# Tile-wise norms, keys turned once, a new loading order, and the scan's output normed and turned inside the projections, in a two-block fp32 kernel

## The reference, cut to what matters

```python
u = modulate(rmsnorm(x, norm1_g), sh1, sc1)              # x: 512 tokens; the same for 256 context tokens
p = u @ w_in
q, k, v, a_raw, beta = gdn_inputs(p, conv_w, rows)       # convolution, silu, l2norm of q and k
o = gdn_bidir(...)                                       # gated delta rule, both directions, 8 heads of 128
z = p[..., Z_OFF:F_OFF]
yb = o * rsqrt(mean(o * o, -1) + EPS) * gdn_norm_g * silu(z)      # per head
yb = yb @ w_gdn_out
ya = fourier_mix(p[..., F_OFF:GA_OFF]) @ w_fourier_out
x = x + g1 * ((sigmoid(ga) * ya + sigmoid(gb) * yb) @ w_merge_out)
h2 = modulate(rmsnorm(x, norm2_g), sh2, sc2)
x = rmsnorm(x + g2 * moe_ffn(h2), final_norm_g)
# second block, two layers: norm, projections, three attentions, projection onto x, norm, feed-forward onto x
# and a last rms_norm
```

## Time and profile before

| | us |
|---|---|
| median of three runs (4345.22 to 4346.45) | 4345.42 |
| the profiled execution | 4341.2 |
| its span in the trace | 4339.3 |

### The profile page before, as it was taken

One profiled execution on the slowest core, in us unless ns is written; L12 is line 12 of the kernel. 1 busy time (PEld: TensorE's weight loads), 2 busy tenths in 40 slices (PEclk: granted clock), 3 DMA queues, 4 the chain that ended last, 5 costly groups with the idle time before them and its releaser, 6 DMA issues. The chain is left out here.

```text
span 4339.3 us, 50934 instructions
## 1 busy us (share of the span) xinstructions
PE 3672.8 (85%) x18705; PEld 3094.1 (71%) x18705; DVE 2828.8 (65%) x3496; ACT 1983.2 (46%) x2560; POOL 300.1 (7%) x316
## 2 busy tenths in 40 slices
PE   2988888888966599999999998378789988678998
PEld 1768888875855488888888886356578776566876
DVE  4686666634453599999999997758555333863323
ACT  3432222222221488888888886218422222662221
POOL 0011111100000101101100000120000000200000
PEclk7988999999977799999999999688889999798999
DMA  3333000014522699999999996630156422112322
GB/s 126 116 117 126 0 1 0 0 60 174 184 84 84 249 372 381 382 379 381 380 381 382 379 380 254 219 84 30 39 168 191 125 70 58 22 64 63 97 93 68
DMA packets 264412, 733.57 MB, mean 169 GB/s; under 512 B 38734, under 2 KB 139710, under 8 KB 211782
## 3 DMA queue, kind: packets, MB, share of 16 engines
q1 hardware_dynamic: 250968, 681.54, 43.2%
q0 software_dynamic: 8416, 32.42, 2.2%
q10 hardware_dynamic: 4896, 17.83, 1.0%
HBM read 684.44 MB, written 52.80 MB: 170 GB/s over the span
## 5 line engine op out<-in xcount | busy, mean ns | idle before, releaser
L1844 DVE TENSOR_TENSOR ex_WP_lo<-ex_W,ex_WP_hi 128x2048 fp32r<-128x2048 f32 x408 | 919.1, 2287 | 42.8 <-ACT ex_WP_hi L1769 38.3
L1769 ACT CAST ex_WP_hi<-ex_W 128x2048 fp32r<-128x2048 f32 x408 | 766.7, 1912 | 178.7 <-PE PS L73 177.8
L71 PE MATMUL PS<-ex_WP_hi,ex_xT_hi 128*128 128x512 f32 x1088 | 428.3, 394 | 16.7 <-DVE ex_WP_lo L1844 8.4
L73 PE MATMUL PS<-ex_WP_hi,ex_xT_lo 128*128 128x512 f32 x1088 | 425.2, 391 | 0.0
L72 PE MATMUL PS<-ex_WP_lo,ex_xT_hi 128*128 128x512 f32 x1088 | 424.7, 390 | 0.0
L71 PE MATMUL PS<-lhT_hi,fu_WP_hi 128*128 128x512 f32 x704 | 280.5, 398 | 20.4 <-DVE fu_WP_lo L2521 20.4
L72 PE MATMUL PS<-lhT_lo,fu_WP_hi 128*128 128x512 f32 x704 | 278.5, 396 | 0.0
L73 PE MATMUL PS<-lhT_hi,fu_WP_lo 128*128 128x512 f32 x704 | 278.1, 395 | 0.0
L71 PEld LDWEIGHTS PS<-ex_WP_hi,ex_xT_hi 128*128 128x128 f32 x1088 | 205.1, 189 | 62.4 <-issue 17.2
L73 PEld LDWEIGHTS PS<-ex_WP_hi,ex_xT_lo 128*128 128x128 f32 x1088 | 204.9, 188 | 43.5
L72 PEld LDWEIGHTS PS<-ex_WP_lo,ex_xT_hi 128*128 128x128 f32 x1088 | 205.2, 189 | 40.7
(11 more groups left out here) (549 smaller groups left out, 8391.1 us busy)
## 6 DMA issues: line engine op xcount, KB each, us to landing
ex_W<-in_w_gate SPq DMA_DIRECT2D x136, 1024.0 KB, 7.3
ex_W<-in_w_up SPq DMA_DIRECT2D x136, 1024.0 KB, 7.7
ex_W<-in_w_down SPq DMA_DIRECT2D x136, 1024.0 KB, 8.1
ringb<-in_w_gu SPq DMA_DIRECT2D x88, 512.0 KB, 4.3
ringb<-in_w_mod SPq DMA_DIRECT2D x72, 512.0 KB, 5.1
ringa<-in_w_mod SPq DMA_DIRECT2D x56, 512.0 KB, 5.0
s_ybuf<-x_sb SPq DMA_DIRECT2D x1, 24576.0 KB, 64.8
ringb<-in_w_down SPq DMA_DIRECT2D x44, 512.0 KB, 3.5
```

Source lines behind the costliest of these rows:

```text
L71: nc.tensor.matmul(out, lhs.hi, rhs.hi, start=start, stop=False)
L73: return nc.tensor.matmul(out, lhs.lo, rhs.hi, start=False, stop=stop)
L1769: nc.scalar.copy(WP.hi[:, c % RP], W[:, c % RAW]).then_inc(s["hi"], 1)
L1844: nc.vector.tensor_tensor(WP.lo[:, c % RP], W[:, c % RAW], WP.hi[:, c % RP].bitcast(F32), ALU.subtract).then_inc(s["lo"][c % RP], 1)
```

## The change

- `m1` loads `w_mod` in eight pieces of 1 MB with five slots, the first ahead of everything else; the nine small loads go to POOL's queue; the context, x (into `x_sb`) and the level table are loaded at its end, and `ldc` is gone (the `cum` table is loaded during `nc`).
- `norm_stage` takes a square root for each tile, PE transposes tile by tile, ACT makes the fp32 value once (`full`, four slots), and the `hi` copies are shared between ACT and DVE; without a split result ACT and DVE share the blocks. `nm`, `n2` and `n3` find their roots made already (`known`), by `square_root` at the end of `mo`, `fn`, `wo` and `fd`; `fn` and `gf` find theirs made in `cb` and `fd`.
- `cl` becomes `by_token_stage`: keys and values of all six chunks are transposed once (72 transposes), and POOL does the clearing.
- `scan_step` has one difference a group and its absolute value (ACT), one exponential in place of two, the row spreads in four banks of their own, beta times v on POOL, no transposes of k and v, and the second half of the attention term after level 0.
- `fft` loads its weights in four parts, with a semaphore each, computes the group norm's scaling of the scan's output beside its matmuls, and loads what `ldg` loaded.
- `zg` starts with z: silu(z) multiplies the scan's output, and the transposes of `yt` follow inside the same stage (`ScanColumns`); all four gated chunks go through `ga`, and four banks serve the chunks. `gn` and `yt` are gone.
- `yb` adds onto `gy` as it comes and turns it at its end (`SumColumns`); `gz` and `mt` are gone.
- extra loads are awaited after the fourth piece.

The diff, cut to its core:

```diff
@@ mod_stage
+            half(0)
             for j, c in enumerate((I["c"][0], I["c_ctx"], I["c_2"][0])):
                 sp.dma_start(cT[:, j, :], column(c)).then_inc(s["small"], 16)
+            half(1)
+            half(2)
             sp.wait_ge(s["zero"], 1)
...
+            for i in range(RAW, 2 * n):
+                sp.wait_ge(s["lo"], i - RAW + 1)
+                half(i)
+            sp.dma_start(C[:, :, :], I["ctx"][0].rearrange("(t p) d -> p t d", p=P)).then_inc(s["x"], 16)
+            sp.dma_start(g.x[:, :, :], I["x"][0].rearrange("(t p) d -> p t d", p=P)).then_inc(s["x"], 16)
+            sp.dma_start(g.lev[:, :, 0:LEVELS, :], I["t_levels"]).then_inc(s["x"], 16)
+            sp.wait_ge(s["x"], 16 * 3)
@@
+def square_root(nc, g, act, t, junk, sem):
+    nc.scalar.activation(junk, g.x[:, t, :], ACT.Square, accum_out=g.ss[:, t:t + 1]).then_inc(sem, 1)
+    act.wait_ge(sem, t + 1)
+    nc.scalar.activation(g.root[:, t:t + 1], g.ss[:, t:t + 1], ACT.Sqrt, bias=g.eps[:, 0:1], scale=1.0 / D)
@@ norm_stage, ACT then DVE
+                if split:
+                    act.wait_ge(s["tr"], k + 1)
+                    if k >= F:
+                        act.wait_ge(s["lo"], k - F + 1)
+                    nc.scalar.activation(full[:, k % F, 0:T], g.PS[:, k, 0:T], ACT.Identity, scale=gain[:, k:k + 1], bias=shift[:, k:k + 1]).then_inc(s["full"], 1)
+                    if k % 2:
+                        high(k - 1)
...
+                    if k % 2:
+                        dve.wait_ge(s["full"], k + 1)
+                        nc.vector.tensor_copy(dst.hi[:, k, :], full[:, k % F, 0:T]).then_inc(s["hid"], 1)
@@ linear_stage
-            if loads and (order["dve"] or mods):
-                dve.wait_ge(s["ex"], 16 * len(loads))
...
+                if p == min(RP - 1, NP - 1) and loads:
+                    dve.wait_ge(s["ex"], 16 * len(loads))
...
+            if residual is not None and residual.roots:
+                for t in range(tiles):
+                    act.wait_ge(s["t"], (nchunks - 1) * tiles + t + 1)
+                    square_root(nc, g, act, t, junk[:, :], s["sq"])
@@ ScanColumns (FROM, BEHIND = 11, 4)
+            for t in range(NT):
+                last = nc.tensor.transpose(g.PS[:, 4 + h % 2, t * P:(t + 1) * P], g.x[:, t, h * P:(h + 1) * P], g.ident[:, :])
@@ scan_step
+            for b, (d, h) in enumerate(BT):
+                act.wait_ge(s["dif"], b + 1)
+                nc.scalar.activation(ea[:, b], ea[:, b], ACT.Abs).then_inc(s["abs"], 1)
+                act.wait_ge(s["abs"], b + 1)
                 nc.scalar.activation(ea[:, b], ea[:, b], ACT.Exp, scale=-1.0).then_inc(s["e"], 1)
+            for b, (d, h) in enumerate(BT):
+                nc.scalar.activation(er[:, b], PS4[:, 2 * b, :, :], ACT.Exp).then_inc(s["er"], 1)
...
+            for d in range(2):
+                nc.gpsimd.tensor_tensor(bv[:, d], qkvT[:, 2 * NQK:, toks[d]], col[:, 0, d, :, None].to_broadcast([P, 8, P]), ALU.mult).then_inc(s["bv"], 1)
+            for b, (d, h) in enumerate(BT):
+                pool.wait_ge(s["e"], b + 1)
+                nc.gpsimd.tensor_tensor(eb[:, b], ea[:, b], g.cum[:, d:d + 1, :].to_broadcast(B4), ALU.mult).then_inc(s["A1"], 1)
...
+                gc = col[:, 1, d, 4 * h:4 * h + 4, None].to_broadcast(B4)
+                nc.vector.tensor_tensor(ea[:, b], PS4[:, 2 * b], gc, ALU.subtract).then_inc(s["dif"], 1)
...
+                    if lv == 0:
+                        act.wait_ge(s["L"], 4 * b + 4)
+                        act.wait_ge(s["A1"], b + 1)
                     nc.scalar.copy(T[:, b], PS4[:, 2 * b, :, :]).then_inc(s["t"], 1)
...
-                pe.wait_ge(s["x"], LEVELS * 4)
+                pe.wait_ge(s["pm"], LEVELS * 4 - 4 + b + 1)
@@ by_token_stage
+            for n, (c, q) in enumerate(groups):
+                for j in range(4):
+                    last = nc.tensor.transpose(g.PS[:, n % 8, j * P:(j + 1) * P], qkvT[:, NQK + 4 * q + j, c * P:(c + 1) * P], g.ident[:, :])
@@ first_half
-            gated_norm_stage(nc, g, oacc, zs)
-            transpose_stage(nc, g, "yt", g.x, uT, lambda k: slice(k * P, (k + 1) * P), lambda k: gn[:, 0:1])
...
-                    nc.vector.tensor_tensor(gy[:, :, :], gy[:, :, :], gb[:, :, :], ALU.add)
-        transpose_stage(nc, g, "mt", gy, uT, lambda k: slice(k, None, KD))
```

More of the change, by code:

```diff
@@ L380, in norm_stage @@
         ss = st.sb("ss", [P, tiles])
-        rt = st.sb("rt", [P, tiles])
+        rt = g.root if known else st.sb("rt", [P, tiles])
         rs = st.sb("rs", [P, tiles])
         xn = st.sb("xn", [P, tiles, D])
-        full = st.sb("full", [P, 2, SEQ])
+        full = st.sb("full", [P, F, SEQ])
         blk = st.block()
@@ L388, in _, with high @@
         def _(act):
-            for t in range(tiles):
-                if t:
-                    act.wait_ge(s["sq"], t)
-                nc.scalar.activation(junk[:, :], src[:, t, :], ACT.Square, accum_out=ss[:, t:t + 1]).then_inc(s["sq"], 1)
-            act.wait_ge(s["sq"], tiles)
-            nc.scalar.activation(rt[:, :], ss[:, :], ACT.Sqrt, bias=g.eps[:, 0:1], scale=1.0 / D).then_inc(s["rt"], 1)
-            for k in range(KD):
-                act.wait_ge(s["tr"], k + 1)
-                out = dst.hi[:, k, :] if isinstance(dst, Pair) else dst[:, k, :]
-                nc.scalar.activation(out, g.PS[:, k, 0:T], ACT.Identity, scale=gain[:, k:k + 1], bias=shift[:, k:k + 1]).then_inc(s["hi"], 1)
+            def high(k):
+                act.wait_ge(s["full"], k + 1)
+                nc.scalar.copy(dst.hi[:, k, :], full[:, k % F, 0:T]).then_inc(s["hia"], 1)
@@ L449, in linear_stage @@
     mods, ring = stream.mods, g.ring
-    banks = 6 if mods else 8
-    with Stage(nc, name, ["piece", "mm", "hi", "done", "act", "dve", "ex", "after", "t"] + (mods.sems if mods else [])) as st:
+    side = side or Side()
+    banks = banks or (6 if mods else 8)
+    with Stage(nc, name, ["piece", "mm", "hi", "done", "act", "dve", "ex", "after", "t", "sq"] + (mods.sems if mods else []) + side.sems) as st:
         s = st.s
@@ L457, in linear_stage @@
             tmp = st.sb("tmp", [P, 2, BANK])
+            if residual.roots:
+                junk = st.sb("junk", [P, D])
+        side.tiles(st)
         items = [(c, t) for c in range(nchunks) for t in range(tiles)]
@@ L1001, in _ @@
+                last.then_inc(s["kk"], 1)
+            for d in range(2):
                 for j in range(4):
-                    last = nc.tensor.matmul(PS4[:, 3 * d + 1, j, :], kT[:, d, j, :], qT[:, d, j, :], start=True, stop=True)
+                    last = nc.tensor.matmul(PS4[:, 2 * d + 5, j, :], kT[:, d, j, :], q_at(d, j), start=True, stop=True)
                 last.then_inc(s["kq"], 1)
@@ L1417, in common @@
     g.silu = sb("silu", [P, 3, KD])
+    g.ss = sb("ss", [P, NT])
+    g.root = sb("root", [P, NT])
     g.bcol = sb("bcol", [P, 3, 6, KD])
@@ L2541, in ffn_down_stage @@
     ring = g.ring
-    with Stage(nc, name, ["hi", "done", "dn", "bank", "t", "t2"]) as st:
+    with Stage(nc, name, ["hi", "done", "dn", "bank", "t", "t2", "sq"]) as st:
         s = st.s
```

628 lines of the change are left out of this document (342 added, 286 removed).

## The result

The changed kernel takes 4151.5 us, median of four runs (4149.8 to 4153.6), beside 4345.3 for the kernel before in the same rounds: 0.956 of it, with an interval of 0.9544 to 0.9574. Forecast were 4140 and a range of 4105 to 4180. Taken again later, it took 4143.3 beside 4341.1, 0.954 (0.9526 to 0.9558). So the gain is 194 to 198 us where 205 were summed.

What follows compares the result with a forecast made beforehand. PE was taken to bound dense stages and the scan's levels, chains through ACT, DVE and loads the other stages. Stage terms summed to -205.5 us, taking 4345.4 to 4140, range 4105 to 4180.

Steps and rivals of the forecast that it cites:

- level 1 later than t+20: Scan step: the prediction called itself wrong if level 1 started later than this; it expected t+16.5.
- The scan's term: Six scan steps: level 1 at t+16.5 instead of t+32.1, 16.4 us saved a step, -99 in all.
- 32 row spreads, PE 6.0: Scan step's beginning: spreads take PE 6.0 us, the fourth difference is done at 6.4, L takes 4.5.
- rival (B): Scan: TensorE stays at 1.2 GHz through the first full level, 17.8 us instead of 8.9; 53 dearer, 4193; chance 0.12.
- the first X 2.5: Scan step's beginning, after L and the masks: the first X takes 2.5 us.
- rival F: Scan: POOL's chain gates level 0's copies; a step loses 5, 4170; half of it 4350 or more; chance 0.02.
- rival D: Scan: Abs and Exp share no ACT table, two loads a group; a step loses 10 us, 4202; chance 0.06.
- rival C: Projections don't take the side work: zg at +16, no gain at yb's tail; 18 more, 4158; chance 0.10.
- The tails: End of yb with gz and mt: eight parts of about 1.0 us each, 14.5 instead of 20.5, -6.
- m1: Stage m1 with its load stage ldc: first cast at about 14, end at about 43.7 instead of 65.6, -22 us.
- The norms: Later norms with known roots start 5.5 us earlier and run faster blocks; the stage before pays 1.5 to 2.
- The extra loads: Waiting for them later lets mo's first difference run earlier, -6 us, and pj's first cast, -5.

Runs made afterwards that it cites:

- kq_pool: Changed kernel with keys-by-queries products behind level 0's first transposes and POOL making only the masked decay before the four X are done: 4131.0 us against 4143.3.
- bv_last: Changed kernel with beta times v moved behind the query products on POOL, ahead of the copies of keys: 4159.7 us in one run.
- fill12: Changed kernel with twelve extra PE transposes at the end of each scan step, into a bank no longer read: 4142.6 us.
- changed kernel again: The changed kernel without an edit, run later as a yardstick in the same rounds as two further versions: 4143.3 us beside 4341.1 for the kernel before.
- best: kq_pool plus twelve transposes at each scan step's end, bias row and c loaded first in m1, and n3 making its own roots: 4122.6 us.
- kk_between: Changed kernel with keys' products after each direction's row spreads, DVE and ACT by direction, keys-by-queries products behind level 0's first transposes: 4144.7 us.
- kq_later: Changed kernel with only the sixteen keys-by-queries records moved behind level 0's first transposes: 4143.0 us.

## Why the prediction held, and where its steps did not

**The stages add up.** The barriers make the span a sum, and every term but the scan's came within 3 us. The scan's part by itself moved the time by 78, where the traces differ by 75. That is why a sum of bounds could hold for a change in so many places. Part of the nearness is luck: the span was 18 off, the median only 11.5, because the profiled run came out 2.1 above the median, where it was assumed 4.2 below. And by its own sign, level 1 later than t+20, the prediction was wrong about the scan: level 1 starts at t+20.3 on average in the first trace, at t+20.0 in the second.

**The scan's term, 99 for 79, failed at two steps of its working.** The first: "32 row spreads, PE 6.0 ..., the fourth difference ... done at 6.4; L 4.5". The 6.0 came from the earlier trace rows, where part of the spreads ran at full clock (358 ns a record); in the last step of the changed kernel all of them run at 1.2 GHz (421 ns, 7.2 busy), but over the six steps of the first trace they read 315 to 421, 376 on average, so that most of the low clock's cost was in the row already. They end at t+6.5 on average, and the fourth difference, 0.7 behind them, at 7.3 (5.9 to 8.2). Then the keys' product, which the sum had left out, stands between the spreads and L: its first eight records put off the first L by another 1.3. L itself takes 4.2, 0.3 less than summed. L ends at 12.8, not at 10.9: 1.9 of the 3.8 that are missing a step. The low clock had been written down as a rival (B), for the whole of level 1. B came true in small part: level 1 ran at 1.2 GHz for up to 4.3 us of a step, 2.9 us of time lost over the six steps in the first trace, where B had 53. The second: "the first X 2.5". By the earlier trace rows DVE's 128x512 instruction with an operand in PSUM takes 692 ns, and X costs that only while POOL is idle. In the changed kernel it took 0.86 to 0.98 on average, and each wait for POOL lengthened PE's pause. From L to level 1 pass 7.5 us instead of the 5.6 summed, the other 1.9: 6.6 with keys by queries out of PE's queue, and 5.4 once POOL keeps away too. So POOL is the larger part of it, 1.2. The two steps show in the table; that POOL is the cause of the second is shown by the run that takes it away (`kq_pool`). That the low clock lengthens the beginning is read from the records (L ends at t+11.5 in the steps where it falls late, at t+13.8 where it falls at once), and no run kept the clock up. Theory 1, which laid the missing time to the clock, had the lesser part.

**POOL (rival F) was named for the wrong reason.** I asked whether POOL's results come late. They never did: the masks are ready by t+10.9 in every step, and level 0 copies at t+15.2 or later. What it did was to hold DVE up, where F had supposed that DVE takes POOL's turns. `bv_last`, which should have been neutral or a gain, cost the scan 22 to 26 us, near the 30 of F, a case that I gave 0.02.

**Abs and Exp (rival D):** no table load stands between L1114 and L1116 in the trace; 630 ns each, back to back. **The projections (rival C):** `zg` took 162.0, against 163.7 by the sum and 176 by the rival.

**The tails.** `yb`, `gz` and `mt` were put at -6 and came to -3.5, with "about 1.0 each" for eight parts; these took 9.8 us from the first cast to the last difference, 1.2 each, and PE's granted clock there is 0.69. **m1:** -22 against -19. The bias row behind three pieces was seen, and the first cast put at 14; it came at 17.5. **The norms** were right in their sums and wrong in their reason. The prediction gave 5.5 to roots made ahead and 1.7 to 2 to the stage that makes them. The run that undoes it shows 0.8 to 2.4 and 1.5 to 3.0. The gain, 4.9 us in an `n3` (22.5 to 17.6 with its own roots), is then left to the order by tiles and the sharing of the blocks, which no run took apart. **The extra loads** were undersized, 11 for 15 to 17.

What stays open: why `fu` (270.3 or 274.6), `yb`, the first `pj` and `wo` take one of two times 1.5 to 4 us apart in traces of kernels that are the same there, and how to keep the clock through a scan step's boundary. The kernel that might be best, the last version with `mt` as a stage of its own, was not run.

## What to carry to other kernels

When stages end in barriers, cut the trace there and sum: the terms hold. Price a moved instruction from a row in which its neighbours are what they will be: the same granted clock, and the same company on POOL. Before giving POOL more to do, look at which DVE instructions read two operands in SBUF at that time, and put POOL's work beside those that read PSUM. Making a value ahead paid only where the stage that makes it had room at its end (`fd`).

## What the runs showed of the hardware

- A DVE instruction with two SBUF operands (128x512, fp32) took 682 ns with POOL idle and 1713 on average beside 128x1024 products and 128x512 copies on POOL (`bv_last`). POOL's product slowed too, from 1.90 to 2.12, and its copy of 128x512 from 0.62 to 1.07 us. Either side can be kept waiting by several instructions of the other in a row: one X took 3.53 (`fill12`), one POOL product of 0.73 took 3.05 (changed kernel again). DVE instructions of the scan step that read an operand in PSUM kept their time beside POOL (128x512: 0.68 to 0.69; L: 0.34) in all these runs.
- Behind a pause of 2.6 to 3.8 us at a step's boundary PE, though busy without a break, falls to 1.2 GHz between the step's start and t+3.1 and comes back at t+9.7 to t+13.5. With the pause cut to 1.4 to 2.3 us it falls at t+2.2 to t+2.9 in five steps of six, and L ends 0.8 earlier on average (`fill12`); in `best`, with the same transposes, it falls at t+0.9 to t+2.9, and L ends 0.3 earlier than in `kq_pool`. It falls once more, at t+16 to t+19, in PE's pause before level 1: in five and three of six steps in the changed kernel's traces, in all six of `fill12` and `bv_last`, and in none of `kk_between`, `kq_later`, `kq_pool` and `best`, which have sixteen more records in that pause.
- A 16 KB load issued behind 3 MB on the same queue landed at 17 us. Issued ahead of them it landed before 7.6, and the 1 MB piece behind it was there at 12.0.
